# Weights of the eighth projection tile rounded earlier, and another order at the outset of a two-block transformer kernel

## What is computed

```python
mod_x = (jax.nn.silu(c) @ w_mod[l] + b_mod[l])[:, None, :]      # 6 x 1024 columns
mod_c = jax.nn.silu(c_ctx) @ w_mod[l] + b_mod[l]
sh1, sc1, gt1, sh2, sc2, gt2 = jnp.split(mod_x, N_MOD, axis=-1)
h_x = _rmsnorm(x, g_pre_mix[l]) * (1 + sc1) + sh1               # 512 tokens
h_c = _rmsnorm(ctx, g_pre_mix[l]) * (1 + csc1) + csh1           # 256 context tokens
u_x, q_x, k_x, v_x = _project(h_x, w_in[l])                     # w_in: 1024 x 2048
...                                                             # pooling and attention
x = x + gt1 * _rmsnorm(mix_x, g_post_mix[l])
...                                                             # MLP, then the second block
```

## Time and profile before

| | us |
|---|---|
| median of 3 runs | 1349.76 (1349.69 to 1350.22) |
| the profiled execution | 1348.28 |
| its span | 1347.0 |
| PE busy in the span | 1328.0 |
| DVE busy | 572.9 |
| ACT busy | 558.5 |
| POOL busy | 627.5 |

### The profile page before, as it was taken

One profiled execution on the slowest core, in us unless ns is written; L12 is line 12 of the kernel. 1 busy time (PEld: TensorE's weight loads), 2 busy tenths in 40 slices (PEclk: granted clock), 3 DMA queues, 4 the chain that ended last, 5 costly groups with the idle time before them and its releaser, 6 DMA issues.

```text
span 1347.0 us, 16436 instructions
## 1 busy us (share of the span) xinstructions
PE 1328.0 (99%) x6562; PEld 1071.7 (80%) x6562; DVE 572.9 (43%) x917; ACT 558.5 (41%) x933; POOL 627.5 (47%) x333
## 2 busy tenths in 40 slices
PE   7999999999999999999999999999999999999999
PEld 4778778878888888888788887766778888888887
DVE  4796785753200052103477656655532221122211
ACT  4532585554332244224565548544543231222220
POOL 2543435943444444555466453632343444444442
PEclk9999999999999999999999999999999999999999
DMA  9575235433333333333342112211232333232231
GB/s 380 220 299 204 84 142 188 141 110 93 96 94 94 102 94 98 106 94 110 110 123 65 48 63 63 64 47 47 63 94 94 94 94 109 94 94 94 94 111 61
DMA packets 41228, 150.70 MB, mean 112 GB/s; under 512 B 4288, under 2 KB 4544, under 8 KB 40384
## 3 DMA queue, kind: packets, MB, share of 16 engines
q1 hardware_dynamic: 40272, 146.36, 33.2%
q0 software_dynamic: 448, 2.62, 0.5%
q10 hardware_dynamic: 432, 0.67, 0.1%
HBM read 146.75 MB, written 2.10 MB: 111 GB/s over the span
## 4 chain that ended last, share of the span: by engine, by line
PE 91%; DVE 4%; ACT 2%; POOL 1%; issue 1%; DMA 0%; DVEq 0%; POOLq 0%; ACTq 0%
PE bank L597 25%; PE bank L599 25%; PE bank L598 25%; PE bank L674 2%; PE bank L1029 2%; PE bank L644 1%; PE bank L646 1%; PE bank L645 1%; PE bank L689 1%; PE bank L658 1%; PE bank L837 1%; PE bank L818 1%; PE bank L682 1%; ACT wH L1337 1%; POOL wL L2708 1%
## 5 line engine op out<-in xcount | busy, mean ns | idle before, releaser
L2708 POOL TENSOR_TENSOR wL<-raw,wH 128x1024 fp32r<-128x1024 f32 (+1 forms) x209 | 508.1, 2433 | 576.6 <-ACT wH L1337 576.5
L597 PE MATMUL bank<-hH,wH 128*128 128x512 f32 x784 | 317.3, 405 | 3.5 <-POOL wL L2708 2.5
L599 PE MATMUL bank<-hH,wL 128*128 128x512 f32 x784 | 306.0, 390 | 0.0
L598 PE MATMUL bank<-hL,wH 128*128 128x512 f32 x784 | 305.7, 390 | 0.0
L1337 ACT ACTIVATE wH<-raw 128x1024 fp32r<-128x1024 f32 (+1 forms) x209 | 219.3, 1051 | 191.0 <-PE bank L599 164.2
L597 PEld LDWEIGHTS bank<-hH,wH 128*128 128x128 f32 x784 | 147.5, 188 | 40.9 <-issue 10.0
L599 PEld LDWEIGHTS bank<-hH,wL 128*128 128x128 f32 x784 | 147.2, 188 | 31.9
L598 PEld LDWEIGHTS bank<-hL,wH 128*128 128x128 f32 x784 | 147.6, 188 | 28.6 <-issue 1.9
L597 PE MATMUL bank<-gH,wH 128*128 128x512 f32 x352 | 137.6, 391 | 0.0
L599 PE MATMUL bank<-gH,wL 128*128 128x512 f32 x352 | 137.0, 389 | 0.0
L598 PE MATMUL bank<-gL,wH 128*128 128x512 f32 x352 | 137.0, 389 | 0.0
(11 more groups left out here) (384 smaller groups left out, 1892.3 us busy)
## 6 DMA issues: line engine op xcount, KB each, us to landing
raw<-in_wall SPq DMA_DIRECT2D x209, 512.0 KB, 3.6
rows<-in_wall SPq DMA_DIRECT2D x24, 1024.0 KB, 11.2
bra<-in_rpbw SPq DMA_DIRECT2D x8, 360.0 KB, 4.5
xq<-in_xt SPq DMA_DIRECT2D x2, 1024.0 KB, 7.0
xT<-in_xn SPq DMA_DIRECT2D x1, 2048.0 KB, 9.0
out_x<-xT SPq DMA_DIRECT2D x8, 256.0 KB, 2.0
vE<-in_ctxt SPq DMA_DIRECT2D x1, 1024.0 KB, 19.7
icn<-in_invc POOLq DMA_DIRECT2D x1, 1024.0 KB, 8.8
```

Source lines behind the costliest of these rows:

```text
L597: matmul(o, a_h, b_h, start=first, stop=False)
L598: matmul(o, a_h, b_l, start=False, stop=False)
L599: return matmul(o, a_l, b_h, start=False, stop=last)
L2708: tt(wL[i % NHL][:, 0:n], raw[i % NRAW][:, 0:n], wH[i % NHL][:, 0:n].bitcast(F32), ALU.subtract).then_inc(s.w_lo, 1)
```

## The change

It has three parts.

1. The chunk of `w_in` tile m = 7 is rounded by an added `ahead("w_in", 7, 6, 2)`: on ACT after `context_high(7)`, ahead of the six evictions of tiles 0 to 5, and on POOL after `first_rest("ctx", 7)`.
2. PE issues 24 matmuls of ones by ones, 128 columns each, into bank 0, before the first sum. `first_rows(0)` stands ahead of the fourth sum (j = 6) and no longer behind it; DVE's `first_vectors(0)` stands ahead of the wait for the root and of `scaled(0)` and `scaled(1)`.
3. `first_coefficients` writes shift to `mod` and scale back into `STAT` by two additions in the place of one, and makes `coef` from `STAT`. The first tile's exact value (j = 0) goes to bank 6 in the place of `tmp`. Bank 7 counts as free for the next columns when `coef` is made.

```diff
-            freed[7] = s.mod_ab, quarter + 1
+            freed[7] = s.coef_a, quarter + 1
...
         pe.wait_ge(s.ones, 3)
+
+        for _ in range(24):
+            matmul(bank[0][:, 0:128], ones[:, :], ones[:, :], start=True, stop=True)
         o = claim(7)
         for j in range(0, 8, 2):
+            if j == 6:
+                first_rows(0)
             pe.wait_ge(s.add_v, ADD_V.x + j // 2 + 1)
             mm = matmul(o, ones[:, :], xsq[:, j, :], start=j == 0, stop=j == 6)
         mm.then_inc(s.summed, 1)
         freed[7] = s.root, logged("x")
-        first_rows(0)
         first_rows(1)
...
         ahead("w_in", 7, 6, 1)
         context_high(6)
         context_high(7)
+        ahead("w_in", 7, 6, 2)
...
-            tt(view(mod[:, f0, :], 0, [[16, 2], [2, 2], [1, 2]]),
-               STAT[:, 0:8].rearrange("p (s j c) -> p s j c", j=2, c=2),
-               view(vcs("b_mod"), f0, [[8, 2], [1, 2], [0, 2]]), ALU.add).then_inc(s.mod_ab, 1)
-            dve.wait_ge(s.mod_ab, quarter + 1)
+            tt(mod[:, f0:f0 + 2, :], STAT[:, 0:4].rearrange("p (j c) -> p j c", c=2),
+               view(vcs("b_mod"), f0, [[1, 2], [0, 2]]), ALU.add).then_inc(s.mod_ab, 1)
+
+            tt(STAT[:, 4:8].rearrange("p (j c) -> p j c", c=2), STAT[:, 4:8].rearrange("p (j c) -> p j c", c=2),
+               view(vcs("b_mod"), 8 + f0, [[1, 2], [0, 2]]), ALU.add).then_inc(s.mod_ab, 1)
+            dve.wait_ge(s.mod_ab, 2 * quarter + 2)
             stt(out=view(coef[:, 0, f0:f0 + 2], 0, [[8, 2], [1, 2]]),
-                in0=view(mod[:, 8 + f0, :], 0, [[1, 2], [2, 2]]), scalar=1.0,
+                in0=view(STAT, 4, [[1, 2], [2, 2]]), scalar=1.0,
...
-                ts(tm[i][:, :], xq[:, j, :], coef[:, 0, j:j + 1], mod[:, j, 0:1], ALU.mult, ALU.add).then_inc(s.full, 1)
+
+                o = tm[i][:, :] if j else bank[6]
+                if j == 0:
+                    dve.wait_ge(s.mod_row, 1)
+                ts(o, xq[:, j, :], coef[:, 0, j:j + 1], mod[:, j, 0:1], ALU.mult, ALU.add).then_inc(s.full, 1)
...
-                    rest(hL[:, j, :], tm[0][:, :], hH[:, j, :], s.rest_v)
+                    rest(hL[:, j, :], o, hH[:, j, :], s.rest_v)
...
+        first_vectors(0)
         dve.wait_ge(s.root, rooted("x"))
         scaled(0)
         scaled(1)
-        first_vectors(0)
         first_coefficients(0)
...
         first_rest("ctx", 7)
+        ahead("w_in", 7, 6, 2)
         for m in range(6, 12):
             ahead("w_in", 7, m)
```

## The result

The changed kernel takes 1344.77 us in the median of seven runs (1344.58 to 1345.10), the kernel before 1349.54 in seven beside it (1348.27 to 1350.22): ratio 0.9968, 95% interval 0.9956 to 0.9979. The profiled execution took 1345.02 (span 1343.7), against 1348.28 (1347.0): 3.3 us less, where the working gave 3.83. So the median fell by more than forecast, 4.8, and the profiled execution by less. Neither difference comes from the two terms of the sum.

What follows compares the result with a forecast made beforehand. PE is busy for 99% of the span, so only its waits, or work that products wait for, can yield a gain. 2.69 + 1.14 = 3.83 us off the median of 1349.76 gives 1345.9, range 1345.0 to 1348.1.

Steps and rivals of the forecast that it cites:

- the two terms of the sum: PE's gains at the eighth tile's weights, 2.69 us, and at the outset, 1.14 us; together 3.83 us.
- The wait at the eighth tile, 2.69: Eighth tile's start: PE's wait for `wL` goes whole, start at 69.37 instead of 72.06, 2.69 us.
- The outset, 1.14: Kernel start: `mrow` copied ahead of the root, first product at 19.93 instead of 21.07, 1.14 us.
- The warm-up: Before the first sum: 24 added matmuls from 1.4 us, full pace from 5.8, done at 8.9.
- That alone buys little: Outset: sums at full speed after the warm-up; root does not move, between 0.3 us earlier and 0.4 later.
- Who starts first holds the memory to the end: DVE's `scaled(1)` against POOL's `wL` at the outset: DVE first by 0.07 us, the other stands.
- None of this is on PE's path later: nothing.: `coef` and first tile in PSUM: worth nothing on PE's path later, except keeping DVE early.
- On SP ... can only help: SP's queue at the eighth tile: next `raw` load comes some 4 us earlier, which can only help.
- 3.83 undiminished to the end: Whole kernel: PE's earlier start at both places should reach the end, profiled execution 1344.45 instead of 1348.28.
- The median of the runs shown is 1.48 above that execution: Kernel before: median 1.48 us above its profiled execution; 3.83 taken from 1349.76 gives 1345.9.

Runs made afterwards that it cites:

- pool_first_2: Changed kernel, with DVE waiting for its first scaling to be written, plus one small instruction, before the second scaling; 1348.52 us, ratio 0.9993.
- coef_sbuf: Changed kernel, with modulation rows written to `mod` in SBUF by one addition and `coef` reading them there, as before; 1347.71 us, ratio 0.9984.
- pool_first: Changed kernel, with three small DVE instructions between its two first scalings; 1344.63 us, ratio 0.9965.
- eighth_only: Kernel before, with only the eighth tile's weights rounded ahead of the pooled evictions; 1345.22 us, ratio 0.9972.
- no_warm: Changed kernel without the 24 warm-up matmuls ahead of the sums; 1345.56 us, ratio 0.9973.
- warm_48: Changed kernel with 48 warm-up matmuls in place of 24; 1348.50 us, ratio 0.9994.
- bias_early: Changed kernel, with bias loads of heads 4 and 5 issued ahead of the six small copies; 1344.22 us, ratio 0.9962; repeated, 1344.52 us, 0.9964.
- mrow_behind: Changed kernel, with DVE's `first_vectors(0)` put back behind `scaled(0)` and `scaled(1)`; 1346.74 us, ratio 0.9980.
- outset_only: Changed kernel, with the eighth tile's weights rounded where they were before; 1346.93 us, ratio 0.9985.
- psum_only: Kernel before, with only the coefficients read from PSUM and the first tile's exact value in PSUM; 1348.22 us, ratio 0.9995.

## Why the prediction was right, and where it was not

- *The wait at the eighth tile, 2.69.* Right: 2.78 (from -1.07 to -3.85). The `wL` undisturbed took 2.40, its cover was 2.8 us, and the ninth tile's was enough.
- *The outset, 1.14.* Right: 1.07, step by step within 0.1 us up to the first product: copy 15.75 (15.71), second scaling 16.96 (16.93) against POOL 17.03 (17.00), `wL` 19.86 (19.83). What it leaves at the end is another matter, see below.
- *The warm-up.* Its end was forecast at 8.9 and is 8.5. The pace changed at 4.7 us and not at 5.8, and that was luck as much as sizing: below. "That alone buys little" held, some 0.4 us.
- *Who starts first holds the memory to the end.* Shown by `pool_first_2` and `coef_sbuf`. By the Trainium skill (SBUF — State Buffer, § Who interferes with whom) a DVE instruction with at most one SBUF input passes, outside the two-port modes; the trace agrees: `coef` from PSUM takes 0.16 in all four quarters, in three of them under a POOL instruction. The traces show the margin of 0.07 held in both profiles of the changed kernel, and one of 0.02 in `pool_first`; no other execution of the two has a time that a flip (3.45 us more in `pool_first_2`) would leave, in twelve and in five.
- *"None of this is on PE's path later: nothing."* Right for the whole change, wrong as a statement on the part: alone it is worth 0.9 us at the eighth tile. The step failed because I took `coef`'s 0.94 us as idle DVE time, while DVE's chain ended the first group.
- *"On SP ... can only help", and 3.83 undiminished to the end.* This step failed. 0.66 us are lost at 163 us, by a stretched SP issue, a late bias and the same lock. The profiled execution came out at 1345.02 and not at 1344.45.
- *"The median of the runs shown is 1.48 above that execution", carried over to the changed kernel.* This failed too, in the other direction, and by more: the median is 1.1 below the forecast. In 34 of 67 executions of the kernel before the mean granted clock is 0.997 to 0.999 and not 1.00, and their medians are 1.6 to 1.9 us above those of the others on the same chip. The changed kernel shows 1.00 in all twelve. Its own profiled execution and its median are 0.25 apart. So the 1.48 was most likely a cost of the kernel before, of the kind that `pool_first_2` shows in its trace: PE stands for about 2.5 us after it had run at 2.4 GHz, and soon after runs at 1.2 for 3.4 us. No trace here shows such an execution of the kernel before, so the place is not shown. What points to the eighth tile's wait: 0 of 6 executions of `eighth_only`, which has the outset of before, against 34 of 67; 1 of 11 and 3 of 11 where the wait is 1.7 and 1.6 us; and 0 of 34 in the other kernels in which PE nowhere stands so long once it has run at 2.4 GHz (`no_warm`, `warm_48`, `pool_first`, `bias_early` twice). The length of the stand alone does not order them: 7 of 11 fell after 1.3 us (`mrow_behind`) and 1 of 11 with 1.7 (`outset_only`).
- *The two misses have opposite signs.* One made the median lower than the sum, the other higher; that the forecast is 1.1 off and not some 1.8 is luck. The two terms were forecast by their mechanism, the median was not.

What stays open: why SP's issue of the six copies is stretched. It took 3.73 us in the traces of the kernel before, of `eighth_only` and of `warm_48`, 4.3 to 5.2 in most others, and in `no_warm` and `psum_only` a `raw` issue behind it was stretched instead. And whether the fall of the clock in the kernel before is at 69 us.

## What to carry over

A wait of PE can cost the clock behind it and is then dearer than it looks in a single profile (1.6 us on top of 2.0 in `pool_first_2`): compare the mean granted clock of all executions before a median is taken as the base of a sum. Parts of a change that shorten the same wait don't add, and an edit that is worth nothing beside another can be worth a microsecond alone. When everything moves earlier, look at what does not move with it on a DMA queue: the loads that are issued last ahead of a tight stage belong in front of the small copies, as early as their buffers are free.

## What the runs showed of the hardware

- The pace of the warm-up matmuls changed from 0.21 to 0.11 us a record at 4.47, 4.67, 4.70, 4.71, 5.32, 5.77, 6.20, 7.03, 7.27 and 7.45 us in ten executions, with the first record at 1.34 in each. The profile's granted clock says 1.00 on both sides of the change (rows of `warm_48`: 11 records in 2 us and then 19, at 1.00), so it has to be read from the distance of the matmuls.
- After a stand of 2.5 us the granted clock does not fall at once: PE ran 1.3 us at full pace, and then 3.4 us at 0.50 (`pool_first_2`).
- Under a POOL instruction that reads and writes SBUF, DVE's tensor_scalar from SBUF to SBUF is held (0.92 us at 39.5 in the changed kernel, in place of 0.55), and the same to PSUM is not: it took 0.81 from 18.13 and ended 0.9 us ahead of POOL's `wL`. So `coef`'s freedom hands the wait to the instruction behind it:

```profile
39.32 0.16 DVE L2051 SCALAR_TENSOR_TENSOR coef<-bank,vecs 128x4 f32<-128x4 f32 x1
39.52 0.92 DVE L2070 TENSOR_SCALAR tmp<-xq,coef,mod 128x512 f32<-128x512 f32 x1
```
